# A decoder layer on one core: unit 0 of the up projection as whole products, new buffer places for the second phase, and a last down chunk with token blocks outermost

## The reference

```python
x = x + merged @ w_out[layer]
h = rms_norm(x, ffn_norm_g[layer])
u, v = jnp.split(h @ w_up[layer], 2, axis=-1)      # w_up: 2048 x 11264
u = causal_dwconv(u, conv_w[layer], conv_b[layer]) # three taps along the tokens
x = x + (jax.nn.gelu(u) * v) @ w_down[layer]       # w_down: 5632 x 2048
return rms_norm(x, final_norm_g)
```

## Time and profile before

| | us |
|---|---|
| median of 3 runs | 2808.55 (2808.36 to 2808.84) |
| the profiled execution | 2806.89 |
| its span, first to last instruction | 2805.1 |
| PE busy in the span | 2751.3 (98%) |
| DVE busy | 1509.0 (54%) |
| ACT busy | 1008.1 (36%) |
| mean granted TensorE clock | 0.992 of full speed |

### The profile page before, as it was taken

How to read it: one execution, slowest core, us unless ns; L and a number is a source line. 1 busy time by engine, 2 the same in 40 slices (tenths; PEclk the granted TensorE clock), 3 DMA queues, 4 the chain that set the end, 5 groups by cost and what they waited for, 6 DMA issues and landing times.

```text
span 2805.1 us, 40745 instructions
## 1 busy us (share of the span) xinstructions
PE 2751.3 (98%) x15945; PEld 2422.0 (86%) x15945; DVE 1509.0 (54%) x1831; ACT 1008.1 (36%) x1237; POOL 187.2 (7%) x156
## 2 busy tenths in 40 slices
PE   8999999999999999999989999999999998999998
PEld 6888888888888888888789999999999987888886
DVE  4445542233333433342487878787878864455454
ACT  4334432222232322132455444555554432122223
POOL 0003310000111000000000000000000000000002
PEclk9999999999999999999999999999999999999999
DMA  6532123334333233343434343535343434333332
GB/s 175 135 103 57 53 75 97 97 92 108 85 82 97 75 102 92 97 143 120 135 94 129 103 132 101 134 101 135 101 131 105 130 131 167 124 115 134 105 113 97
DMA packets 421668, 308.89 MB, mean 110 GB/s; under 512 B 6469, under 2 KB 367574, under 8 KB 420969
## 3 DMA queue, kind: packets, MB, share of 16 engines
q1 hardware_dynamic: 415351, 295.83, 36.7%
q10 hardware_dynamic: 5826, 10.76, 1.1%
q0 software_dynamic: 432, 1.50, 0.2%
HBM read 288.09 MB, written 22.06 MB: 111 GB/s over the span
## 4 chain that ended last, share of the span: by engine, by line
PE 93%; DVE 2%; issue 2%; ACT 1%; DMA 1%; SPq 0%; POOL 0%; ACTq 0%; DVEq 0%; POOLq 0%
PE bank L889 31%; PE bank L528 19%; PE bank L530 19%; PE bank L529 19%; PE bank L719 2%; PE bank L713 1%; DMA x_in<-in_x_dram 0%; DMA a_dram<-v_sb 0%; DVE ring_lo L1717 0%; ACT l_win L1081 0%; ACT l_slc L1081 0%; PE bank L769 0%; POOL l_slc L1952 0%; SPq L362 0%; PE bank L868 0%
## 5 line engine op out<-in xcount | busy, mean ns | idle before, releaser
L528 PE MATMUL bank<-h_hi,w_hi 128*128 128x512 f32 x1216 | 481.3, 396 | 2.8 <-DVE w_lo L1419 2.8
L530 PE MATMUL bank<-h_hi,w_lo 128*128 128x512 f32 x1216 | 474.6, 390 | 0.0
L529 PE MATMUL bank<-h_lo,w_hi 128*128 128x512 f32 x1216 | 474.3, 390 | 0.0
L889 PE MATMUL bank<-t_hi,ring_hi 128*128 128x256 f32 x1408 | 401.4, 285 | 18.6 <-DVE ring_lo L1717 18.6
L889 PE MATMUL bank<-t_hi,ring_lo 128*128 128x256 f32 x1408 | 400.5, 284 | 0.0
L1409 DVE TENSOR_TENSOR w_lo<-w_raw,w_hi 128x2048 fp32r<-128x2048 f32 x105 | 240.7, 2292 | 262.0 <-ACT w_hi L983 261.7
L983 ACT ACTIVATE w_hi<-w_raw 128x2048 fp32r<-128x2048 f32 x105 | 200.8, 1912 | 424.7 <-PE bank L530 420.6
L889 PE MATMUL bank<-m32r,ring_hi 128*128 128x256 f32 x1408 | 327.5, 284 | 0.0
L889 PEld LDWEIGHTS bank<-t_hi,ring_hi 128*128 128x128 f32 x1408 | 272.6, 194 | 19.6 <-issue 19.6
L528 PE MATMUL bank<-d_hi,a_hi 128*128 128x512 f32 x704 | 275.0, 391 | 7.9 <-DVE x L1889 7.9
L529 PE MATMUL bank<-d_lo,a_hi 128*128 128x512 f32 x704 | 274.7, 390 | 0.0
(11 more groups left out here) (283 smaller groups left out, 4883.1 us busy)
## 6 DMA issues: line engine op xcount, KB each, us to landing
w_raw<-in_w_in_dram SPq DMA_DIRECT2D x76, 1024.0 KB, 5.7
raw<-in_w_up_dram SPq DMA_DIRECT2D x44, 1024.0 KB, 6.9
raw<-in_w_up_dram SPq DMA_DIRECT2D x88, 512.0 KB, 6.2
d_raw<-in_w_down_dram SPq DMA_DIRECT2D x44, 1024.0 KB, 5.1
w_raw<-in_w_out_dram SPq DMA_DIRECT2D x16, 1024.0 KB, 5.1
a_dram<-v_sb SPq DMA_DIRECT2D x44, 256.0 KB, 2.0
a_in<-a_dram SPq DMA_DIRECT2D x11, 1024.0 KB, 7.4
w_raw<-in_w_branch_nsa_dram SPq DMA_DIRECT2D x8, 1024.0 KB, 5.7
```

What stands on the lines that cost most here:

```text
L528: mm(dst, l_hi, r_hi, start=first, stop=False)
L529: mm(dst, l_hi, r_lo, start=False, stop=False)
L530: return mm(dst, l_lo, r_hi, start=False, stop=final)
L889: last = mm(pb[bank][:, 0:TH], left[:, w], right[:, k, :], start=first and k == 0 and left is ring_hi[b] and right is y_hi, stop=k == KH - ...
```

## The change

- **Unit 0.** Its seven products go. Two slots `S_UP` and `S_UP + 1` are added, loaded, split and multiplied like those of phase 1: 128 columns of v and 128 of u against the whole normed activation, in `h_hi` and `h_lo`. These are the four quarters and their splits at the same time (`h2_hi`, `h2_lo`), 4 of 16 blocks at a time, three of the four steps during the output projection. Between parts of the two slots PE does the transposes of group 3 and of rstd. DVE copies the two banks out whole. There are 7 x 43 = 301 products in the place of 308.
- **Blocks of the activations.** y11, y21, y22 are views of `h_hi`/`h_lo`; only t1, t2, t3, t4 are made apart, partly in place over `m32` and over the quarter y12 of `h`.
- **Buffers.** `raw`, the ring, `s_a`, `s_3`, `u_sb`, `v_sb`, `d_raw`, `d_hi`, `d_lo`, `a_in`, `a_hi`, `a_lo`, `gfin`, `sq3`, `rs_rep2` lie elsewhere. Column groups 0 and 1 of the old `x1` are read back into `xs`, which is apart from `x1`.
- **End of phase 2.** ACT and DVE take the last two pieces between the steps for the down projection. The loads of `xs` and of the second block of `a` stand ahead of the last product's end.
- **Last chunk.** Its four slots of weights are split ahead into four places (`tail_hi`, `tail_lo`). PE then goes by token block, and by column group within it; squares, gain, scale and store follow by token block.

```diff
-S_DN = S_WO + 16
+S_UP = S_WO + 16
+S_DN = S_UP + 2
-PRODUCTS = 7 * UNITS
+PRODUCTS = 7 * (UNITS - 1)
...
@@ SP
-        load_v(unit(0))
-        load_u(unit(0), 0)
-        load_u(unit(0), 1)
-        sp.wait_ge(w_ready, S_DN + 2)
         load_v(unit(1))
-        sp.wait_ge(w_used, S_DN + 2)
         load_u(unit(1), 0)
         load_u(unit(1), 1)
+        load_cols(slot(S_UP), wup, D_FF)
+        load_cols(slot(S_UP + 1), wup, 0)
+        sp.wait_ge(w_ready, S_UP + 1 + 3)
+        load_v(unit(2))
+        load_u(unit(2), 0)
+        load_u(unit(2), 1)
...
+        sp.wait_ge(s_add, 4 * (UNITS - 1))
         sp.wait_ge(a_out, 16 * 8 + 64)
-        sp.wait_ge(prod_done, unit(43).q + 4)
         load_a(0, 0)
+        store_a(unit(41))
+        sp.wait_ge(piece_ok, PRODUCTS)
+        sp.wait_ge(x1_put, 80)
+        sp.dma_start(xs[0][:], x1_d[:, :, 0:512]).then_inc(x_loaded[0], 16)
+        sp.wait_ge(prod_done, PRODUCTS - 2)
+        sp.dma_start(xs[1][:], x1_d[:, :, 512:1024]).then_inc(x_loaded[1], 16)
         load_a(1, 1)
-        store_a(unit(41))
         sp.wait_ge(prod_done, PRODUCTS)
-        sp.wait_ge(x1_put, 80)
-        for j in range(4):
+        for j in range(2, 4):
             sp.dma_start(x1[:, :, 512 * j:512 * j + 512], x1_d[...]).then_inc(x_loaded[j], 16)
         store_a(unit(42))
         store_a(unit(43))
...
@@ PE
+        pe.wait_ge(hl_ok, 3)
+        pe.wait_ge(x1_add, 14)
+        slot_cols(up_v, 0, range(0, 8))
         x1_transposes(3)
+        slot_cols(up_v, 0, range(8, 12))
+        slot_cols(up_u, 1, range(0, 8)).then_inc(y12_used, 1)
+        pe.wait_ge(rep2_ok, 1)
         pe.wait_ge(x1t_read, 20)
         for t in range(TOK):
             last = mm(pb[5][:, t * P:t * P + P], rs_rep2[:, t, :], ident[:], start=True, stop=True)
         last.then_inc(rbc2_ps, 1)
+        slot_cols(up_u, 1, range(8, 12))
+        pe.wait_ge(hl_ok, 4)
+        slot_cols(up_v, 0, range(12, KT))
+        slot_cols(up_u, 1, range(12, KT))
...
+        pe.wait_ge(a_ok, CHUNKS)
+        for t in range(TOK):
+            for j in range(4):
+                if t == 0:
+                    pe.wait_ge(w_ready, S_DN + 4 * (CHUNKS - 1) + j + 3)
+                pe.wait_ge(dn_add, 16 * (CHUNKS - 1) + 4 * t + j + 1)
+                ...  # 12 matmuls with tail_hi[j], tail_lo[j] into bank_d[j]
...
@@ DVE, start of phase 2
+        for sub in range(1, 4):
             lo(slot(S_WO + 12 + sub + 1))
+            h2_lo(sub - 1)
+            if sub == 2:
+                V.tensor_tensor(r11, r12, r11, ALU.subtract).then_inc(t_add, 1)
+            if sub == 3:
+                y_lo_part(1, t1[:, 1], r11, t1[:, 0])
+        wo_add(3, S_UP - 1)
+        lo(slot(S_UP + 1))
+        piece(0, 0, x_of(m, 0, 0))
+        add_s1(m, (x1_add, 16))
+        h2_lo(3)
+        ...  # rstd, rs_rep2
+        V.tensor_tensor(r11, r22, r11, ALU.subtract).then_inc(t_add, 1)
+        V.tensor_tensor(r12, r22, r12, ALU.subtract).then_inc(t_add, 1)
+        piece(1, 1, x_of(m, 0, 1))
+        V.tensor_tensor(r21, r21, r11, ALU.subtract).then_inc(t_add, 1)
+        link(V.tensor_copy(rbc[:], pb[5][:]))
+        piece(2, 2, s_a[1][:])
+        add_s2(m, 3)
+        y_lo_part(2, t2_lo, r11, t2_hi)
+        V.tensor_copy(v_sb[:, 0, :], pb[0][:]).then_inc(c12_out, 1)
+        V.tensor_tensor(u_sb[:, 0, :], pb[1][:], rbc[:], ALU.mult).then_inc(c21_out, 1)
+        piece(3, 3, s_a[1][:])
+        add_s4(m, 4)
+        y_lo_part(3, t3_lo, r12, t3_hi)
+        y_lo_part(4, t4_lo, r21, t4_hi)
...
@@ DVE, end of phase 2
+        piece(PRODUCTS - 2, (PRODUCTS - 2) % RING, x_of(before, 1, 1))
+        add_tap1(unit(UNITS - 2))
         down_lo(slot(S_DN))
+        piece(PRODUCTS - 1, (PRODUCTS - 1) % RING, s_a[1][:])
+        add_tap0(unit(UNITS - 2))
         a_low(0, 0)
-        period(UNITS)
+        out_c21(before, PRODUCTS - 1)
+        out_c12(before, PRODUCTS)
+        add_tap1(before)
+        add_tap0(before)
...
@@ ACT, end of phase 2
+        piece_x(PRODUCTS - 2, (PRODUCTS - 2) % RING, last, 1, 1)
+        act.wait_ge(prod_done, last.q + 3)
         down_hi(slot(S_DN))
+        piece_s(PRODUCTS - 1, (PRODUCTS - 1) % RING, last, s_a[1], 3)
+        gelu(unit(UNITS - 2))
+        act.wait_ge(prod_done, last.q + 6)
         a_high(0, 0, 16)
-        period(UNITS)
-        gelu(unit(43))
+        taps(last)
+        gelu(last)
```

More of the change, by code:

```diff
@@ L195, in build @@
+    ring_at = [A_ + 32 * KB, Y_, 80 * KB, 96 * KB]
     ring_hi = [at(f"ring_hi{b}", ring_at[b], [P, KH * P], F32R) for b in range(RING)]
     ring_lo = [at(f"ring_lo{b}", ring_at[b] + 4 * KB, [P, KH * P], F32R) for b in range(RING)]
[L197 to L200, removed]
+    s_a = [at(f"s_a{b}", Y_ + 8 * KB + b * 4 * KB, [P, KH * P]) for b in range(2)]
@@ new lines, in build @@
+    t3_hi, t3_lo = hl[:, 0, 0:KH, TH:SEQ], hl[:, 1, 0:KH, TH:SEQ]
+    t4_hi, t4_lo = m32r[:, 0:KH, TH:SEQ], m32r[:, KH:KT, 0:TH]
+    y11 = [hl[:, z, 0:KH, 0:TH] for z in range(2)]
+    y21 = [hl[:, z, KH:KT, 0:TH] for z in range(2)]
+    y22 = [hl[:, z, KH:KT, TH:SEQ] for z in range(2)]
+    t1_, t2_ = [t1[:, z] for z in range(2)], [t2_hi, t2_lo]
+    t3_, t4_ = [t3_hi, t3_lo], [t4_hi, t4_lo]
+    d_raw = at("d_raw", 64 * KB, [P, 2, 2048])
+    d_hi = [at("d_hi0", A_, [P, 2048], F32R), at("d_hi1", 0, [P, 2048], F32R)]
@@ L458, in period @@
             if r <= UNITS - 3:
-                hold(sp, s_add, now.n * 4 + 4)
+                hold(sp, s_add, now.n * 4)
                 load_v(unit(r + 2, i))
@@ L469, in _ @@
                 period(r, i)
+        period(42)
         def load_down(s, c, j):
@@ L880, in _, with product @@
             wo_slot(S_WO + 12 + sub, 0, None, sub, None)
-        def product(q, b, y_hi, y_lo, bank, first):
+        def product(q, b, y, bank, first):
             pe.wait_ge(piece_ok, q + 1)
@@ L937, in period @@
-            product(now.q + 6, (b + 2) % RING, t3_hi, t3_lo, bank_a[par], False)
+                pe.wait_ge(y_part, 2)
+            product(now.q + 3, (b + 3) % RING, t2_, bank_a[par], False)
+            if r >= 2:
+                pe.wait_ge(c22_out, now.n)
+                product(now.q + 4, b % RING, t4_, bank_a[1 - par], False)
+                pe.wait_ge(p5_out, now.n)
+                product(now.q + 5, (b + 1) % RING, y22, bank_c[1 - par], False)
+            pe.wait_ge(u2_out, now.n + 1)
@@ L939, in _ @@
+            if r == 1:
+                pe.wait_ge(y_part, 3)
+            last = unit(r + 1, i).q - 1
+            product(last, (last if i is None else b + 6) % RING, t3_, bank_a[par], False)
+            if r < UNITS - 1:
+                pe.wait_ge(c12_out if r == 1 else c21_out, 1 if r == 1 else now.n)
         period(1)
+        pe.wait_ge(y_part, 4)
         with pe.Fori(0, 10) as i:
@@ L1220, in _, with y_hi_part, h2_hi @@
         own.leave(3)
-        def y_hi_part(dst, src, adds=None):
-            if adds is not None:
-                act.wait_ge(t_add, adds)
+        def y_hi_part(dst, src, adds):
+            act.wait_ge(t_add, adds)
             A(dst, src, ACT.Copy).then_inc(yh_part, 1)
+        def h2_hi(q):
+            A(h_hi[:, 4 * q:4 * q + 4, :], m32[:, 4 * q:4 * q + 4, :], ACT.Copy).then_inc(hh_ok, 1)
         def piece(q, b, src):
@@ L1841, in period @@
+            add_s3(now)
             if r >= 2:
+                piece(now.q + 4, (b + 4) % RING, x_of(before, 1, 1))
+            out_c11(now, now.q + 2)
+            if r >= 2:
+                piece(now.q + 5, (b + 5) % RING, s_a[1 - par][:])
                 add_tap1(unit(r - 2, i))
-            if r < UNITS:
-                piece(now.q + 6, (b + 6) % RING, s_3[:])
+            m = unit(r + 1, i)
+            piece(m.q - 1, (m.q - 1 if i is None else b + 6) % RING, s_3[:])
             if r >= 2:
@@ L1921, in _ @@
         for t in range(TOK):
-            down_add(slot(tail + 3), CHUNKS - 1, 3, [t])
-            if t:
-                final_scale(t - 1)
-            dve.wait_ge(sq3_done, 12 + t + 1)
+            for j in range(4):
+                dve.wait_ge(dn_done, 12 * (CHUNKS - 1) + 4 * t + j + 1)
+                d = x1[:, t, 512 * j:512 * j + 512]
+                V.scalar_tensor_tensor(d, pb[(5, 6, 7, 0)[j]][:], rr[:, t:t + 1], d, ALU.mult, ALU.add).then_inc(dn_add, 1)
+                if j == 1 and t:
+                    final_scale(t - 1)
+            dve.wait_ge(sq3_done, 4 * t + 4)
             link(V.tensor_reduce(mx[:, t:t + 1], ss.rearrange("p (g t) -> p t g", t=TOK)[:, t, :], AX.X, ALU.add))
```

376 lines of the change are left out of this document (168 added, 208 removed).

## The result

Four runs of the changed kernel gave a median of 2787.32 us (2786.18 to 2787.96), four of the kernel before on the same chip 2808.45 (2808.35 to 2808.84): a ratio of 0.9924, 95% interval 0.9907 to 0.9941. The profiled execution took 2786.82 us, its span is 2785.0 (2805.1 before). In the page of the profile after, busy times and chain have hardly moved; the gain does not show there, and has to be looked for by stretches.

What follows compares the result with a forecast made beforehand. PE, busy in 98% of the span, was taken as the bound, so only its few waits and the end could be won. Gains of 11.4 + 5.1 + 3.4 = 19.9 us gave 2788.6 us, range 2784 to 2795 (8 in 10).

Steps and rivals of the forecast that it cites:

- Part A: Start of phase 2: PE starts with blocks that need no sums, DVE's list becomes the bound; gain 11.4 us.
- +1.6 us for whole products: Unit 0 as slots: PE's own work grows by 1.6 us, 21.8 us against 20.2 for seven products.
- Part B: From the last ring pieces to the third down slot: the chain of transfers starts earlier; gain 5.1 us.
- Part C: The end behind the last matmul: adds follow PE by token block, last store alone in queue; gain 3.4 us.
- the queue: Rival, 17%: ahead of the third down slot, loads moved together slow down, leaving 1.1 of 5.1 us; 2792.6 us.
- The clock did fall: Rival, 10%: at phase 2's start the clock falls in shorter gaps, twice 2 us instead of 0.5; about 2792.
- the queue is no bound: Rival, 6%: the store ahead of the third down slot gets through early, PE's work bounds there; 2783.2 us.
- Strided rows: Rival, 4%: products reading 1 KB rows at 2 KB stride have longer matmuls; at 5 ns each 36 us, 2825.

Runs made afterwards that it cites:

- Ten more matmuls: Changed kernel with ten more 512-column matmuls on PE in unit 0, into a bank that nobody reads: 2787.47 us.
- the swapped banks: Changed kernel with DVE emptying unit 0's two banks ahead of the low part of t2 instead of behind it: 2786.12 us.
- the copies: Version with third down slot's weights loaded ahead of x and a's high part ahead of gelu, plus rbc and v_sb copies moved from DVE to ACT: 2777.18 us.
- old last chunk: Changed kernel with its last chunk by column group again, with the old splits, adds, squares and gains: 2792.10 us.

## Why the prediction came out

2788.6 was forecast and 2787.3 measured; the three terms were 11.4, 5.1 and 3.4 us, and the profiles show 11.85, 4.16 and 3.65, with 0.4 between the third down slot and PE's end that was in no term. For the profiled execution 2787.0 was forecast and 2786.8 measured. That this is so close is luck in part: the errors are +0.45, -0.94, +0.25 and +0.43, and they cancel. The median came lower still, since it lies 0.5 us above the profiled execution and not 1.7 as before.

- **Part A, 11.4: mechanism right, 0.5 short.** The first slot started without a wait; PE waited 0.3 us for `rs_rep2` (0.6 forecast); its waits are 0.3 + 2.09 + 2.07 = 4.5 us and not 6.7. Half clock took the place of most of the rest: products 1 to 3, 72 matmuls, took 10.33 us in the place of 8.64, so the clock cost 1.7 us, where 0.5 was put for the whole stretch. Either way product 4 started at 1427.42 (1427.3 forecast) and product 5 at about 1430.3 (1430.7 forecast), since neither PE's work nor its clock bounds this stretch but DVE's list. The forecast's own step that failed is small: it added 0.5 us for the clock behind a stretch that its list bounds, and the clock was not on the path. Ten more matmuls and the swapped banks (S unchanged) and the copies (S 1.10 shorter) show that bound. No run has unit 0, the new views or the earlier splits by themselves, so how the 11.85 us divide among these is not shown.
- **+1.6 us for whole products: not on the path.** The rows' 0.227 and 0.120 us held: 7058 matmuls in 846.95 us. But the term decides nothing here.
- **Part B, 5.1: the mis-sized term, 4.16.** The chain was the right one: store, wait on SP, weights, splits. The loads were asked for at E + 6.1 (6.2 forecast), and the store landed at 2304.5, E + 27.2 (26.7 forecast): 6.82 MB in 21.15 us, 0.322 MB/us for the 0.333 put. From landing to PE it took 12.85 us in the place of 12.4: 0.3 more until the weight load was issued (0.37 us of "issue" in the chain, 0.07 before) and 0.15 more for the load (5.25 and 5.10). The waits at E were 2.20 (2.0 forecast), none ahead of piece 300 (1.3 forecast) and 2.08 (2.8 forecast): behind the first wait the clock fell, to 0.62 from 2279.4 to 2283.9, which stretched product 299 over the time until piece 300 was there. In the kernel with the old last chunk the clock held, and the waits were 2.21, 0.89 and 2.46, near the forecast. The down projection started at E + 11.76 (11.9), the third slot at E + 40.08 (39.1) with a wait of 4.64 (5.4).
- **Part C, 3.4: 3.65.** 8.85 us from PE's end, 9.1 forecast; the last store landed in 3.9 us as the earlier trace rows. PE did not wait in the last chunk. The old order alone brings the 12.5 back.
- **The rivals.** Of the 5.1 us the queue took 0.65 back, not 4. The clock did fall, behind the wait that ended at 1415.02, and by nearly the 2 us priced for a fall, but in a stretch that PE does not bound. That the queue is no bound is disproved by the third slot's wait and by what its removal gave. Strided rows cost nothing: 0.120 us a matmul, 7058 without a break.

## What to carry to other kernels

Cut two profiles at events that both have, and compare stretch by stretch: here most stretches repeat to some hundredths of a us, while totals move by 1 to 2 us with a part that nobody touched. Ask of each wait of the busy engine whether a later one covers it: while the third slot waited for transfers, PE's coming 1.0 us sooner gave nothing; once it did not, a wait of 2.08 us less was worth 4.0. GpSimd was no free helper for VectorE beside passes over SBUF: the move cost 1.7 to 3.3 us. Copies moved to ScalarE made the stretch 1.1 us shorter.

## What the runs showed of the hardware

- TensorE's clock can fall to its 1.2 GHz level (granted clock 0.50) behind short waits of a busy engine, and not each time. In the twelve executions it fell behind all 13 waits of 2.99 us and more from the start of unit 0 on, and behind none of the 10 of 0.35 to 1.28 us. Between these it goes by chance or by something that the traces don't show: the 2.1 us wait behind product 0 was followed by a fall in 4 of 5 executions, the one of 2.04 to 2.07 us ahead of product 4 in none of 4, that of 2.5 us at the same place in 2 of 5, the 2.2 us at E in 10 of 11, and 2.05 to 2.46 us ahead of the down projection in 6 of 7. The fall need not come at once: in the changed kernel PE was back at work at 1415.02, and up to 1416.00 eight matmuls still had a granted clock of 1.00. A fall cost PE 1.3 us (L, old last chunk) to 2.9 us (21 matmuls in 7.67 us behind the third slot's wait there).
- A step of VectorE on four columns was held up for 4.35 us by one GpSimd instruction, and a pass of 1024 columns for 4.41 us. Where VectorE's pass had started first, GpSimd's took 6.48 us in the place of 4.54: the order of issue decided who waited.
